# The head of a hybrid encoder layer: two loads of x on ScalarE's queue, transposes moved behind products, one zero product more

## Chip, cores and metric

One core of one Trainium2 chip. The metric is the device time of one execution in microseconds (us). The kernel is written in the direct style: each engine has its own program, and semaphores order them.

## What is computed

One layer (DEPTH = 1) of an encoder over 512 tokens of 1024 channels, in float32: RMS norm, one projection `h @ w_in` to 7 blocks of 512 columns and 3072 gate logits, three branches (chunked softmax attention, stick-breaking attention, multi-scale pooling), a gated sum through `w_out`, then a gated MLP with a convolution of width 3.

```
def rms_norm(x, gain):
    y = xf * lax.rsqrt(jnp.mean(xf * xf, axis=-1, keepdims=True) + EPS)
    return (y * gain.astype(jnp.float32)).astype(x.dtype)
...
        h = rms_norm(x, norm_mix[l])
        proj = h @ w_in[l]
        q_a, k_a, v_a, q_b, k_b, v_b, u_c, g_logits = jnp.split(proj, IN_SPLITS, axis=-1)
...
        x = x + merged @ w_out[l]
        h2 = rms_norm(x, norm_ffn[l])
        x = x + conv_gated_mlp(h2, w_up[l], conv_w[l], conv_b[l], w_down[l])
```

## The kernel before

Every large product is made of three matmuls in the type float32r. Both operands are split into a high part (a copy rounded to float32r, by ACT) and a low part (the rest, by DVE), and `product` (L1607 to L1611) adds hi x lo, hi x hi and lo x hi in PSUM. Weights come in units of 128 x 1024 floats, 512 KB, through two slots of `w_raw`: SP loads a unit in two transfers, ACT writes `w_hi`, DVE writes `w_lo` and counts up `lo_ready`, and PE waits for that.

Only the **head**, the first 24 us or so, is touched. There x has no transposed form yet. x lies in `x_in` as four blocks of 128 tokens (t = 0 to 3), and each block is loaded in two halves of 512 channels (g = 0 and 1), 256 KB each (`x_load`, L291 to L294), with a semaphore of its own, `x_landed[t][g]`. PE transposes a half with four matmuls against the identity (`x_transposes`, L1638 to L1647), ACT copies the result to `xt_hi` (`xt_split_hi`, L544), DVE writes `xt_lo` (`xt_split_lo`, L985).

The first products are those of the values of branch A, with the transposed x as the stationary operand. The first unit holds two slices of 512 columns of `w_in`, for channels 0 to 127 and 128 to 255. Here they are called the **first and the second slice**. The first is one transfer (L313, semaphore `first_landed`), the second two transfers of 64 partitions each (L315). ACT multiplies each with the norm's gain on its way to `w_hi` (`first_hi`, L563), DVE does the same for `w_lo` (`first_lo`, L991). For token block 0, PE needs the first slice for `kk = 0` and the second for `kk = 1`; token blocks 1 to 3 follow with two products each.

The order of each engine is written out by hand. PE: three zero products (`warm(0)`, zeros from `h_lo` into a bank that is written over later), the transposition of the gains, the transposes of block 0, three more zero products (`warm(1)`, count in `WARM`), the transposes of block 1, and then in turn product and transposes, so that the sets of blocks 2 and 3 follow the first and second product of block 0. ACT: load of the gains (`g_row`, L537), table load, first slice, block 0, second slice, blocks 1 to 3. DVE: `g_mix`, first slice, block 0, second slice, blocks 1 to 3. SP issues all other loads: block 0 of x, first slice, second slice, blocks 1 to 3, the next unit, the second halves of x, and, when DVE has done the second slice (`lo_ready` at 1), the unit after that.

Of the kernel before, what the change touches and what calls it, by code (L numbers as in the profile page):

```python
# [22 lines left out]
TT = S // P  # L23
# [4 lines left out]
WB = 512  # L28
# [44 lines left out]
QK0_BANK, SS0_BANK = 2, 4  # L73
SS_BANK = 6
MIX = 4
WARM = (3, 3)


def build(nc, x, norm_mix, w_in, b_gate, q_norm_a, k_norm_a, rel_bias_a, w_pool, pool_scale,
          w_branch_a, w_branch_b, w_branch_c, w_out, norm_ffn, w_up, conv_w, conv_b, w_down, out):  # L80
    ctx = ExitStack()
    with ctx:
# [3 lines left out]
        def sem(name):  # L86
            return ctx.enter_context(nc.semaphore(name))

        def region(kb, *specs):


            with ExitStack() as scope:
                if kb:
                    scope.enter_context(nc.sbuf_tensor(f"below_{specs[0][0]}", [P, 256 * kb], FP32))
                return [scope.enter_context(nc.sbuf_tensor(n, s, d)) for n, s, d in specs]
# [36 lines left out]
        x_in, = region(64, ("x_in", [P, TT, D], FP32))  # L132
# [51 lines left out]
        x_landed = [[sem(f"x_landed{t}_{g}") for g in range(2)] for t in range(TT)]  # L184
# [62 lines left out]
        def x_turned(t):  # L247

            return ps[:, X_BANKS[t], :].rearrange("p (k c) -> p k c", c=P)
# [22 lines left out]
        xw = x[0].rearrange("(t p) d -> p t d", p=P)  # L272
# [17 lines left out]
        def _(sp):  # L290
            def x_load(t, g):  # L291

                c = slice(g * WB, g * WB + WB)
                sp.dma_start(x_in[:, t, c], xw[:, t, c]).then_inc(x_landed[t][g], 16)  # L294
# [13 lines left out]
            def values(n, u, c0):  # L308
                load(n, u % 2, [win_c[:, 2 * u + i:2 * u + i + 1, c0:c0 + WB] for i in range(2)])
# [3 lines left out]
            sp.dma_start(w_raw[:, 0, 0:WB], win_v0[:, 0, :]).then_inc(first_landed, 16)  # L313
            for r in (slice(0, HD), slice(HD, P)):
                sp.dma_start(w_raw[r, 0, WB:UNIT], win_v0[r, 1, :]).then_inc(w_landed[0], 16)  # L315
            for t in range(1, TT):
                x_load(t, 0)
            values(N_VA + 1, 1, V_A * P)
            for t in range(TT):
                x_load(t, 1)  # L320
# [200 lines left out]
        def _(act_e):  # L521
            a = act_e
# [12 lines left out]
                act(w_hi[:, slot, :], w_raw[:, slot, :], ACT.Copy).then_inc(hi_ready, 1)  # L535

            a.dma_start(g_row[:, :], norm_mix[0].rearrange("(k c) -> k c", c=P)).then_inc(gmix_landed, 16)  # L537
            a.preload_act_table_set("natural_log_exp_and_others")
            a.wait_ge(const_ready, 1)

# [1063 lines left out]
        def _(pe):  # L1604
# [21 lines left out]
            def warm(i):  # L1626


                for _ in range(WARM[i]):
                    mm3(ps[:, V_A_BANKS[0], :], ones_heads[:, :], h_lo[:, 0, :], start=True, stop=True)  # L1630
# [7 lines left out]
            def x_transposes(t, g):  # L1638

                pe.wait_ge(x_landed[t][g], 16)  # L1640
                if g == 1:
                    pe.wait_ge(xt_lo_ready, t + 1)
                if (t, g) == (2, 0):
                    pe.wait_ge(gmix_ready, 1)
                for k in range(4 * g, 4 * g + 4):
                    last = nc.tensor.transpose(x_turned(t)[:, k % 4, :], x_in[:, t, k * P:k * P + P], ident[:, :])  # L1646
                last.then_inc(xt_rest_done if g else xt_done, 1)  # L1647

            def value_product(bank, k, t, c, slot):

                tk = slice(t * P, t * P + P)
                return product(ps[:, bank, :], xt_hi[:, k, tk], xt_lo[:, k, tk], w_hi[:, slot, c], w_lo[:, slot, c],
                               k == 0, k == KD - 1)
# [10 lines left out]

            x_transposes(0, 0)
            warm(1)
            x_transposes(1, 0)
            for t in range(TT):
                pe.wait_ge(xt_lo_ready, t + 1)
                for kk in range(2):  # L1670
                    if t == 0:
                        pe.wait_ge(lo_ready if kk else first_lo_ready, 1)
                    last = value_product(V_A_BANKS[t], kk, t, slice(kk * WB, kk * WB + WB), 0)
                    if t == 0:
                        x_transposes(kk + 2, 0)
            last.then_inc(unit_done, 1)
            for t in range(TT):
                x_transposes(t, 1)
# [353 lines left out]
```

## Time and profile before

| | us |
|---|---|
| median of 3 runs | 823.93 (823.73 to 824.07) |
| profiled execution, device time | 822.09 |
| its span, first to last instruction | 820.2 |
| PE busy | 813.5 |
| DVE busy | 606.3 |
| ACT busy | 407.4 |
| DMA, mean rate | 138 GB/s |

The span is 1.9 us shorter than the profiled execution's device time. Times inside the trace are counted from the start of the span. Busy time of PE is that of matmuls, which overlap in the pipeline; where a line has a start, the distance between two starts says what a matmul takes.

### The profile page before, as it was taken

How to read it: one execution, taken by the hardware profiler on the slowest of the kernel's cores; microseconds unless marked ns; L12 is line 12 of the kernel's file. 1: busy time of each engine (PE TensorE's matmuls, PEld its weight loads, DVE VectorE, ACT ScalarE, POOL GpSimd, SP SyncE). 2: the span in 40 equal slices, each digit the busy share in tenths (PEclk: the TensorE clock that was granted, in tenths of full speed). 3: DMA queues.
4: the chain of work that ended last, by engine and by line, in shares of the span. 5: the costliest groups of instructions: out<-in, count | busy, mean ns of one | idle time of the engine just before them, and what ended most of it. 6: DMA issues, size and time to landing. Idle time of an engine off the chain costs nothing.

```text
span 820.2 us, 11715 instructions
## 1 busy us (share of the span) xinstructions
PE 813.5 (99%) x3863; PEld 675.8 (82%) x3863; DVE 606.3 (74%) x893; ACT 407.4 (50%) x572; POOL 24.1 (3%) x42
## 2 busy tenths in 40 slices
PE   8999999999999999999999999999999999999998
PEld 6888888888888888888888888888888888888886
DVE  5958888868668775555554578777777878898797
ACT  6547676656545545434341464334433444565653
POOL 1010000000000060000000000000000000000000
PEclk9999999999999999999999999999999999999999
DMA  6342333222222223333367523665655555576454
GB/s 210 103 130 78 96 85 100 80 63 67 77 77 77 69 73 90 102 91 102 90 219 245 190 78 103 205 193 191 201 190 188 180 185 188 172 221 210 149 182 173
DMA packets 130702, 113.26 MB, mean 138 GB/s; under 512 B 6148, under 2 KB 109544, under 8 KB 129264
## 3 DMA queue, kind: packets, MB, share of 16 engines
q1 hardware_dynamic: 129840, 110.63, 43.0%
q0 software_dynamic: 672, 2.12, 0.9%
q8 instruction: 16, 0.26, 0.1%
q10 hardware_dynamic: 160, 0.14, 0.0%
q14 instruction: 14, 0.11, 0.0%
HBM read 99.21 MB, written 13.65 MB: 138 GB/s over the span
## 4 chain that ended last, share of the span: by engine, by line
PE 98%; DMA 1%; DVE 0%; SPq 0%; issue 0%; DVEq 0%
PE ps L1609 30%; PE ps L1610 30%; PE ps L1611 30%; PE ps L1741 2%; PE ps L1731 2%; PE ps L1756 1%; PE ps L1755 1%; DMA x_in<-in_x_dram 1%; PE ps L1909 0%; DVE out_sb L1594 0%; PE ps L1646 0%; PE ps L1705 0%; PE ps L1724 0%; PE ps L1706 0%; SPq L315 0%
## 5 line engine op out<-in xcount | busy, mean ns | idle before, releaser
L1609 PE MATMUL ps<-h_lo,w_hi 128*128 128x512 f32 x704 | 276.6, 393 | 0.1
L1611 PE MATMUL ps<-h_hi,w_lo 128*128 128x512 f32 x704 | 274.1, 389 | 0.0
L1610 PE MATMUL ps<-h_hi,w_hi 128*128 128x512 f32 x704 | 274.1, 389 | 0.0
L971 DVE TENSOR_TENSOR w_lo<-w_raw,w_hi 128x1024 fp32r<-128x1024 f32 x112 | 138.0, 1232 | 108.0 <-ACT w_hi L535 79.2
L535 ACT ACTIVATE w_hi<-w_raw 128x1024 fp32r<-128x1024 f32 x96 | 101.7, 1060 | 201.7 <-PE ps L1611 201.6
L1611 PEld LDWEIGHTS ps<-h_hi,w_lo 128*128 128x128 f32 x704 | 132.2, 188 | 27.9
L1609 PEld LDWEIGHTS ps<-h_lo,w_hi 128*128 128x128 f32 x704 | 132.2, 188 | 27.4 <-issue 0.3
L1610 PEld LDWEIGHTS ps<-h_hi,w_hi 128*128 128x128 f32 x704 | 132.3, 188 | 26.3
L1456 DVE TENSOR_TENSOR conv_in<-ps,r_ffn 128x512 f32<-128x512 f32 x44 | 30.3, 690 | 23.9 <-PE ps L1611 22.1
L890 ACT ACTIVATE conv_out<-conv_in,par 128x512 f32<-128x512 f32 x44 | 35.5, 806 | 9.7 <-DVE conv_in L1456 9.7
L1444 DVE SCALAR_TENSOR_TENSOR conv_out<-conv_in,par,conv_out 128x512 f32<-128x512 f32 x44 | 33.1, 752 | 5.0 <-DVE conv_out L1441 1.1
L1441 DVE SCALAR_TENSOR_TENSOR conv_out<-conv_in,par,conv_out 128x512 f32<-128x512 f32 x44 | 32.8, 746 | 1.0 <-ACT conv_out L890 0.9
L529 ACT ACTIVATE w_hi<-w_raw 128x1024 fp32r<-128x1024 f32 x16 | 16.9, 1058 | 29.3 <-PE ps L1611 29.3
L1609 PE MATMUL ps<-w_lo,a_hi 128*128 128x512 f32 x78 | 30.4, 389 | 0.0
L1610 PE MATMUL ps<-w_hi,a_hi 128*128 128x512 f32 x78 | 30.4, 389 | 0.0
L1611 PE MATMUL ps<-w_hi,a_lo 128*128 128x512 f32 x78 | 30.3, 389 | 0.0
L1609 PE MATMUL ps<-h_lo,a_hi 128*128 128x512 f32 x76 | 29.6, 389 | 0.0
L1610 PE MATMUL ps<-h_hi,a_hi 128*128 128x512 f32 x76 | 29.6, 389 | 0.0
L1611 PE MATMUL ps<-h_hi,a_lo 128*128 128x512 f32 x76 | 29.6, 389 | 0.0
L1173 DVE TENSOR_TENSOR pt_lo<-ps,pt_hi 128x1280 fp32r<-128x1280 f32 x16 | 23.9, 1491 | 6.1 <-ACT pt_hi L683 5.9
L1146 DVE TENSOR_TENSOR_SCAN suffix<-keep 128x512 f32<-128x512 f32 (+3 forms) x32 | 23.8, 807 | 4.4 <-ACT keep L667 4.2
L1500 DVE TENSOR_TENSOR w_lo<-w_raw,w_hi 128x1024 fp32r<-128x1024 f32 (+1 forms) x22 | 24.2, 1100 | 3.0 <-ACT w_hi L908 3.0
(238 smaller groups left out, 1304.1 us busy)
## 6 DMA issues: line engine op xcount, KB each, us to landing
w_raw<-in_w_in_dram SPq DMA_DIRECT2D x103, 256.0 KB, 3.1
w_raw<-in_w_up_dram SPq DMA_DIRECT2D x88, 256.0 KB, 3.2
raw_t<-in_w_down_dram SPq DMA_DIRECT2D x11, 1024.0 KB, 8.7
down_sums<-t_sum SPq DMA_DIRECT2D x11, 1024.0 KB, 5.7
w_raw<-in_w_down_dram SPq DMA_DIRECT2D x33, 256.0 KB, 3.0
w_raw<-down_sums SPq DMA_DIRECT2D x33, 256.0 KB, 3.9
w_raw<-in_w_out_dram SPq DMA_DIRECT2D x16, 256.0 KB, 3.2
w_raw<-down_sums SPq DMA_DIRECT2D x22, 128.0 KB, 3.0
```

The lines of the kernel that those rows point to most:

```text
L535: act(w_hi[:, slot, :], w_raw[:, slot, :], ACT.Copy).then_inc(hi_ready, 1)
L890: act(conv_out[:, e, :], conv_in[:, e, 2:2 + S], ACT.Identity, scale=pcol(CW2, j + KF * gv), bias=pcol(CB, j + KF * gv)).then_inc(tap_init, 1)
L971: v.tensor_tensor(w_lo[:, slot, :], w_raw[:, slot, :], r32(w_hi[:, slot, :]), ALU.subtract)\
L1146: last = v.tensor_tensor_scan(rev(suffix, e, n), rev(keep[h], c, n), rev(keep[h], c, n), 1.0, ALU.mult, ALU.bypass)
L1173: v.tensor_tensor(pt_lo[:, :], scores_of(h, 0, SCORES), r32(pt_hi[:, :]), ALU.subtract).then_inc(pt_lo_ready, 1)
L1441: v.scalar_tensor_tensor(out=conv_out[:, e, :], in0=conv_in[:, e, 1:1 + S], scalar=pcol(CW1, j + KF * gv), in1=conv_out[:, e, :], op0=ALU. ...
L1444: v.scalar_tensor_tensor(out=conv_out[:, e, :], in0=conv_in[:, e, 0:S], scalar=pcol(CW0, j + KF * gv), in1=conv_out[:, e, :], op0=ALU.mult ...
L1456: v.tensor_tensor(conv_in[:, e, 2:2 + S], ps[:, e, :], r_ffn[:, :], ALU.mult).then_inc(cin_ready, 1)
L1500: v.tensor_tensor(d_wlo[e][:, u, 0:wide], d_raw[e][:, u, 0:wide], r32(d_whi[e][:, u, 0:wide]), ALU.subtract)\
L1609: mm3(dst, l_hi, r_lo, start=start, stop=False, **kw)
L1610: mm3(dst, l_hi, r_hi, start=False, stop=False, **kw)
L1611: return mm3(dst, l_lo, r_hi, start=False, stop=stop, **kw)
```

## The change

SP no longer issues the first halves of blocks 1 and 2 of x; ACT issues them, behind its load of the gains and ahead of its table load. On PE the transposes of block 1 go behind the first product, and those of blocks 2 and 3 both behind the second. The second batch of zero products has four in place of three.

```
-WARM = (3, 3)
+WARM = (3, 4)
...
-            for t in range(1, TT):
-                x_load(t, 0)
+            x_load(3, 0)
...
             a.dma_start(g_row[:, :], norm_mix[0].rearrange("(k c) -> k c", c=P)).then_inc(gmix_landed, 16)
+
+            for t in (1, 2):
+                a.dma_start(x_in[:, t, 0:WB], xw[:, t, 0:WB]).then_inc(x_landed[t][0], 16)
             a.preload_act_table_set("natural_log_exp_and_others")
...
             warm(1)
-            x_transposes(1, 0)
             for t in range(TT):
                 pe.wait_ge(xt_lo_ready, t + 1)
                 for kk in range(2):
                     if t == 0:
                         pe.wait_ge(lo_ready if kk else first_lo_ready, 1)
                     last = value_product(V_A_BANKS[t], kk, t, slice(kk * WB, kk * WB + WB), 0)
-                    if t == 0:
-                        x_transposes(kk + 2, 0)
+                    if t == 0 and kk == 0:
+                        x_transposes(1, 0)
+                    elif t == 0:
+                        x_transposes(2, 0)
+                        x_transposes(3, 0)
```

PE's order at the start of the program, before. The rows with `ones_heads` are zero products, those with `ident,x_in` are the four transposes of one block, and three rows with `xt_hi` or `xt_lo` are one product:

```order
L1630 MATMUL ps<-h_lo,ones_heads 128x512 x3
L1646 MATMUL ps<-ident,x_in 128x128 x4
L1609 MATMUL ps<-w_lo,xt_hi 128x512
L1610 MATMUL ps<-w_hi,xt_hi 128x512
L1611 MATMUL ps<-w_hi,xt_lo 128x512
L1646 MATMUL ps<-ident,x_in 128x128 x4
L1609 MATMUL ps<-w_lo,xt_hi 128x512
L1610 MATMUL ps<-w_hi,xt_hi 128x512
L1611 MATMUL ps<-w_hi,xt_lo 128x512
L1646 MATMUL ps<-ident,x_in 128x128 x4
```

The same place with the change (lines of the changed kernel are two higher there):

```order
L1632 MATMUL ps<-h_lo,ones_heads 128x512 x4
L1611 MATMUL ps<-w_lo,xt_hi 128x512
L1612 MATMUL ps<-w_hi,xt_hi 128x512
L1613 MATMUL ps<-w_hi,xt_lo 128x512
L1648 MATMUL ps<-ident,x_in 128x128 x4
L1611 MATMUL ps<-w_lo,xt_hi 128x512
L1612 MATMUL ps<-w_hi,xt_hi 128x512
L1613 MATMUL ps<-w_hi,xt_lo 128x512
L1648 MATMUL ps<-ident,x_in 128x128 x8
```

The first product no longer stands behind the transposes of block 1, and the second has one set of transposes ahead of it instead of two.

SP's order at the start, before (L294 is x, L313 the first slice, L315 the second, L303 units):

```order
L294 DMA x_in<-in_x_dram 128x512
L313 DMA w_raw<-in_w_in_dram 128x512
L315 DMA w_raw<-in_w_in_dram 64x512 x2
L294 DMA x_in<-in_x_dram 128x512 x3
L303 DMA w_raw<-in_w_in_dram 128x512 x2
```

ACT's order at the start with the change (L539 is new; L565 splits the slices, L546 the blocks of x):

```order
L536 DMA g_row<-in_norm_mix_dram 8x128
L539 DMA x_in<-in_x_dram 128x512 x2
L540 ACT_TABLE_LOAD
L565 ACTIVATE w_hi<-w_raw,g_mix 128x512
L546 ACTIVATE xt_hi<-ps 128x4x128
L565 ACTIVATE w_hi<-w_raw,g_mix 128x512
```

SP's three loads of x behind the slices become one, and ACT has the two others ahead of its table load.

## Rows read from the trace of the kernel before

**Rows 1.** The page: busy time of the engines, and the chain that ended last.

```profile
PE 813.5 (99%) x3863; PEld 675.8 (82%) x3863; DVE 606.3 (74%) x893; ACT 407.4 (50%) x572; POOL 24.1 (3%) x42
...
PE 98%; DMA 1%; DVE 0%; SPq 0%; issue 0%; DVEq 0%
```

**Rows 2.** Stretches: length, busy PE, PEld, DVE, ACT, POOL; granted clock, DMA share, GB/s.

```profile
2.19:7.30 5.11, 4.17 (x11) 2.58 (x11) 1.52 (x3) 2.40 (x4) 0.78 (x3) 1.00 0.86 273
7.30:24.00 16.70, 16.70 (x88) 14.20 (x89) 12.36 (x24) 12.76 (x24) 0.00 (x0) 1.00 0.61 205
24.00:820.00 796.00, 792.65 (x3766) 659.01 (x3764) 591.50 (x863) 391.61 (x545) 22.06 (x27) 1.00 0.44 136
```

**Rows 3.** What PE waited for: total us, times, longest.

```profile
PE ps L1646 <- DMA x_in<-in_x_dram: 0.9, 1, 0.9
```

**Rows 4.** Timeline of PE: start, us, instruction, idle time before it.

```profile
7.30 0.66 PE L1646 MATMUL ps<-ident,x_in 128*128 128x128 f32 x4 [0.94 <-DMA x_in<-in_x_dram]
7.72 0.47 PE L1609 MATMUL ps<-w_lo,xt_hi 128*128 128x512 f32 x1
8.03 0.39 PE L1610 MATMUL ps<-w_hi,xt_hi 128*128 128x512 f32 x1
8.26 0.40 PE L1611 MATMUL ps<-w_hi,xt_lo 128*128 128x512 f32 x1
...
8.85 0.47 PE L1609 MATMUL ps<-w_lo,xt_hi 128*128 128x512 f32 x1
```

**Rows 5.** Timeline of ACT, the same columns.

```profile
0.88 0.60 ACTq L537 DMA_DIRECT2D g_row<-in_norm_mix_dram  x1
1.51 1.28 ACT L538 ACT_TABLE_LOAD   x1 [1.51 <-PEq L2022]
4.83 0.72 ACT L563 ACTIVATE w_hi<-w_raw,g_mix 128x512 fp32r<-128x512 f32 x1 [2.03 <-DMA w_raw<-in_w_in_dram]
...
6.71 0.72 ACT L563 ACTIVATE w_hi<-w_raw,g_mix 128x512 fp32r<-128x512 f32 x1 [0.68 <-DMA w_raw<-in_w_in_dram]
8.00 0.60 ACT L544 ACTIVATE xt_hi<-ps 128x512 fp32r<-128x512 f32 x1 [0.57 <-PE ps L1646]
```

**Rows 6.** Timeline of DVE.

```profile
6.34 0.69 DVE L985 TENSOR_TENSOR xt_lo<-ps,xt_hi 128x512 fp32r<-128x512 f32 x1
7.46 0.75 DVE L991 SCALAR_TENSOR_TENSOR w_lo<-w_raw,g_mix,w_hi 128x512 fp32r<-128x512 f32 x1 [0.44 <-ACT w_hi L563]
```

**Rows 7.** Timeline of SP, its issues; the last two from windows inside one issue.

```profile
1.34 0.42 SPq L313 DMA_DIRECT2D w_raw<-in_w_in_dram  x1
1.81 1.20 SPq L315 DMA_DIRECT2D w_raw<-in_w_in_dram  x2
...
3.06 0.59 SPq L294 DMA_DIRECT2D x_in<-in_x_dram  x1
...
3.69 0.43 SPq L294 DMA_DIRECT2D x_in<-in_x_dram  x1
```

**Rows 8.** Issues one by one, us to landing: x blocks 1, 2; second slice's halves.

```profile
x_in<-in_x_dram SPq DMA_DIRECT2D x1, 256.0 KB, 4.2
...
w_raw<-in_w_in_dram SPq DMA_DIRECT2D x1, 128.0 KB, 3.2
...
w_raw<-in_w_in_dram SPq DMA_DIRECT2D x1, 128.0 KB, 4.3
```

**Rows 9.** Timeline of PE, the zero products of the second batch.

```profile
5.31 1.05 PE L1630 MATMUL ps<-h_lo,ones_heads 128*128 128x512 f32 x2
...
5.74 0.63 PE L1630 MATMUL ps<-h_lo,ones_heads 128*128 128x512 f32 x1
```

**Rows 10.** Stretches of the DMA, the columns of rows 2.

```profile
2.50:2.75 0.25, 0.25 (x1) 0.19 (x1) 0.00 (x0) 0.25 (x1) 0.25 (x2) 1.00 0.98 369
2.75:3.00 0.25, 0.25 (x2) 0.22 (x1) 0.00 (x0) 0.05 (x1) 0.23 (x1) 1.00 0.79 230
3.00:3.25 0.25, 0.25 (x2) 0.11 (x1) 0.00 (x0) 0.00 (x0) 0.00 (x0) 1.00 0.67 213
...
4.25:5.25 1.00, 1.00 (x5) 0.96 (x5) 0.00 (x0) 0.42 (x1) 0.00 (x0) 1.00 0.74 96
```

## Prediction

> **What bounds the kernel now.** I read the profile page first. PE is busy for 813.5 of 820.2 us and the chain that ended last is 98% PE [rows 1], so only time in which PE stands still, or work added to it, can move the end. Next I read the table by stretches [rows 2]. From 7.30 to 24 us PE is busy for all 16.70 us, and after 24 us it is idle for 796.00 - 792.65 = 3.35 us in all. The idle time that an edit of the head can reach is therefore ahead of 7.30 us. The list of what PE waited for agrees: behind the kernel's first instructions it has one entry, 0.9 us for a piece of x [rows 3]. The change is about that one. A shift of PE's work at 7.30 us arrives at the end one for one, because nothing behind it waits for anything but PE.
>
> The third view is the timeline of PE, ACT and DVE up to 10 us [rows 4 to 6]. The reader is to see two chains in it. **Chain one**: the first slice of w_raw lands and ACT splits it at 4.83 and block 0 of x behind it, DVE starts its lo part at 6.34 and ends it at 6.34 + 0.69 = 7.03. From about 7.05 (an engine starts some 0.02 to 0.03 after its releaser) PE has all it needs for the first product, but it stands at the transposes of block 1, whose x lands only at 7.26 (issued at 3.06, 4.2 to landing [rows 7, 8]). **Chain two**: the second slice lands, ACT starts on it at 6.71, DVE works from 7.46 to 7.46 + 0.75 = 8.21, and only then may the second product run.
>
> **The change on PE.** Two matmuls of a product start 0.23 apart (8.03 and 8.26), so a product takes 3 x 0.23 = 0.69; from one product to the next, with a set of four transposes between them, it is 8.85 - 7.72 = 1.13, which leaves 0.44 for the set [rows 4]. Nothing is added there but the zero product, and nothing is removed; the order alone changes. Let d be the time by which the first slice lands later than before, and e the same for the second slice.
> - PE starts the first product at 7.05 + d in place of the transposes at 7.30.
> - The transposes of block 1 start at 7.74 + d and take 0.66 to their end at 8.40 + d. ACT needs 0.04 + 0.60, DVE 0.03 + 0.69 and PE 0.03, so the third product may start at 9.79 + d.
> - The second product starts at the later of 7.05 + d + 0.69 + 0.44 = 8.18 + d and 8.21 + e. Behind it are 0.69 and two sets of transposes, 0.88, so the third product may also not start before 9.75 + d or 9.78 + e.
> - Before, the third product started at 9.97 (read off the second at 8.85, with 0.69 + 0.44 behind it).
>
> So PE's whole stream moves by the larger of **d - 0.18 and e - 0.19**. The most that can be won is 0.18 us, with d = e = 0; the idle time of 0.94 that the trace shows can't be won whole, since chain one ends at 7.03 whatever x does.
>
> **The zero product.** The second and third zero product of the second batch start at 5.31 and 5.74, and the last one takes 0.63 [rows 9]. The spacing of 0.43 against the 0.23 of the same shape after 7.30 says that PE works at the 1.2 GHz level there and at 2.4 GHz from 7.30 on (the column of the granted clock shows 1.00 in both stretches, so it has no record of the first one [rows 2]). A fourth one would start near 6.16 and end by 6.80, or sooner if the clock rises ahead of it. It lies in the gap up to 7.05 and costs nothing; if the cover were gone it would cost 0.43.
>
> **The two loads.** SP loses two issues (0.59 and 0.43 [rows 7]); all that stands behind them on SP is issued about 1.0 us earlier. ACT gets them behind its load of the gains (0.88 to 1.48), so at about 1.5 and 2.0, where SP had them at 3.06 and 3.69. Queued behind them on ACT is the table load, 1.28, which would end at about 2.5 + 1.28 = 3.8 in place of 2.79. It is hidden: ACT then waits 2.03 for the first slice until 4.83 [rows 5]. Should each issue take the 0.60 of the gains' load, it ends at 4.0, still hidden.
>
> What the two loads do to d and e is the unknown. Before, the first slice (issued by SP at 1.34) had only block 0 of x ahead of it, and the second slice (two issues from 1.81 on [rows 7]) nothing of x behind the first slice. Now 256 KB of block 1 are asked for at 1.5, and 256 KB of block 2 at 2.0, in the same time. At the best rate here, 369 GB/s, 256 KB are 0.71 us [rows 10]. **Bounds of d**: none (the second queue is served behind), and 0.71 (all of block 1 goes ahead). The DMA was not full from 2.75 to 3.25 (230 and 213 GB/s [rows 10]), which leaves room for some 70 KB, 0.2 us. I take d = 0.45, near the upper end less that room. **Bounds of e**: none, and the time until block 2 landed before, since by then the same five transfers were all in: 3.69 + 4.2 = 7.89 [rows 8] against 6.71, so 1.2; with both blocks wholly ahead and today's slow stretch unchanged, 1.4. The slow stretch from 4.25 to 5.25, where the DMA is 74% busy but moves 96 GB/s, lies on the second slice: its second half landed 4.3 us after its issue, its first 3.2 [rows 8, 10]. A part of block 2 can move during it at no cost to the slice. I take e = 0.5, in the lower half for that reason.
>
> The rows show no case of two queues that are both full, so they can't say who is served first. The Trainium skill ("DMA: Bandwidth & Descriptors", Queues, rings and completion order) says that each DMA engine takes turns between the queues that have work for it, packet by packet, and the section on issuing engines adds that a second issuing engine saves only the time of issuing. That speaks against this change: by it both transfers of equal size end together, d is at its upper end of about 0.7 and the sum would be 0.5 instead of 0.3. No row here tests it.
>
> **Behind the head.** The other loads of SP, the second halves of x and the next unit among them, are issued 1.0 us earlier and have no more bytes ahead of them than they had; PE waits for none of them up to 24 us [rows 2], and it needs them 0.2 us earlier at most. The unit after that is behind the same wait as before, the second slice's lo part on DVE, and moves by e. Cost: nothing.
>
> **Sum.** The larger of 0.45 - 0.18 = 0.27 and 0.5 - 0.19 = 0.31: PE's stream is 0.3 us later. The profiled execution took 822.09 us, span 820.2, so the same execution with the change would take 822.4. The median of the runs shown is 823.93, 1.84 above it; the same 0.3 on it gives **824.2 us**. Bounds by the unknowns: 823.75 (no delay) to 825.1 (e = 1.4). A difference of 0.2%, 1.65 us, is about what a measurement of this kernel can tell from no change, so nearly all of this is "the same".
>
> **Rivals.**
> - **No delay at all, or the second queue does nothing of what it should** (it is served only when SP's has no work): 823.75, within 0.2%. For it: ACT's loads are asked for later than the first slice. Against: both are in flight together, at a DMA that is 98% busy [rows 10]. 24%.
> - **Long delay of the second slice**: by the skill's turns and with block 2 wholly ahead, shifts of 0.8 to 1.6 us, up to 825.5; within 0.2%. 15%.
> - **Slower**, one mechanism: the second slice waits behind both blocks (1.4) and a second slow stretch as that at 4.25 falls on it, worth the 4.3 - 3.2 = 1.1 us that today's one shows. e = 2.5, and the time is 823.93 + 2.3 = 826.2. It decides from e = 1.85 on (1.65 + 0.19 us). For it: such a stretch is there in the only trace. Against: one has to come on top. 6%.
> - **Faster through the clock.** In the trace the clock is up by 7.30, behind an idle gap of 0.94. The timed runs are 1.84 us longer than the profiled one. Were that because PE stays at 1.2 GHz for longer in them (about eight matmuls of the head at 0.43 in place of 0.23 are 1.6), the fourth zero product and the shorter gap could give it back: 823.93 - 1.84 = 822.1. The skill ("TensorE: Matmul & The Clock Gate", Part 1) says that the clock rises after sustained work and that the moment varies from run to run, which would allow it. Against: the three runs lie within 0.34 us, where a moment that varied would scatter them. 5%.
>
> **Chances.** The forecast's case, a shift of 0.05 to 0.8 us, has 50%; with 24% and 15% beside it, the same within 0.2% has 89%, slower 6%, faster 5%. Range for 8 in 10: from the no-delay case less the scatter of the runs (some 0.3 to 0.4) to the middle of the long-delay case: 823.3 to 825.3.
>
> **What would show it.** In the profile of the changed kernel: PE's first product stands ahead of the transposes of block 1 and starts between 7.1 and 7.8, not at 7.72 behind them; ACT's first split starts at 4.83 + d with d from 0 to 0.71; its second at 6.71 + e; four zero products end ahead of the first product; PE's wait for x is gone, and a wait for DVE's w_lo or xt_lo stands in its place. The end shifts by the larger of d - 0.18 and e - 0.19. I am wrong if PE waits later than 10 us in the head, if block 0 of x lands late behind ACT's loads, or if the time moves by over 1.6 us with this stretch unchanged.

## The result and the profile after

The median of 22 executions is 824.94 us (823.19 to 827.18), that of the kernel before, run beside it, 823.73 us (821.89 to 824.36). The ratio is 1.0018 with a 95% interval of 1.001 to 1.0026, or 0.8 to 2.1 us: slower, by about 0.2%. That is clear of the noise, and at the edge of what the prediction called the same. This ratio and those below lie nearer to the ratio of the means (824.77 against 823.29 here) than to that of the medians; for a kernel whose executions fall into groups, as will be seen, the median jumps when one group passes a half. The profiled execution took 825.44 us (span 823.6), against 822.09 and 820.2 before.

Both sets of executions are wider than the three that stood ahead of the prediction. The kernel before falls into two groups. Of 33 executions measured with the first experiments, 11 lie from 821.9 to 822.4 and 22 from 823.4 to 824.3, with nothing between. The profiled execution of before belongs to the lower group, and all three runs of the table to the upper one. With the change, 7 executions lie from 823.2 to 823.9, 4 from 824.3 to 824.8 and 11 above 825; 10 of these 11 have a mean granted clock of 0.997 or 0.998, which none of before had in the experiments below. In other sets a few executions of before do lie between the groups (822.58 and 822.67 among the 22 above).

The stretches after, with the same columns as [rows 2]:

```profile
2.19:7.30 5.11, 4.60 (x12) 2.91 (x12) 1.31 (x3) 2.49 (x3) 0.77 (x3) 1.00 0.96 278
7.30:24.00 16.70, 15.26 (x73) 12.82 (x74) 9.37 (x15) 11.50 (x21) 0.00 (x0) 0.90 0.51 173
24.00:823.60 799.60, 795.99 (x3781) 661.68 (x3779) 594.98 (x874) 393.18 (x549) 22.32 (x27) 1.00 0.44 136
```

Up to 24 us PE is idle for 1.44 us where it was idle for nothing, and the granted clock is 0.90 in that stretch. After 24 us PE is idle for 3.6 us, where it was 3.4. Where the clock was low is shown by a stretch of its own:

```profile
10.46:13.87 3.41, 3.41 (x13) 2.92 (x12) 0.91 (x2) 1.19 (x3) 0.00 (x0) 0.50 0.98 349
```

From 10.46 to 13.87 us the granted clock is 0.50, that is 1.2 GHz, with PE busy all the time. Ahead of it PE had stood still twice. The list of what PE waited for, against [rows 3]:

```profile
PE ps L1611 <- DVE w_lo L993: 1.2, 1, 1.2
PE ps L1611 <- DVE xt_lo L987: 0.8, 1, 0.8
```

PE's timeline, against [rows 4]:

```profile
4.74 2.06 PE L1632 MATMUL ps<-h_lo,ones_heads 128*128 128x512 f32 x4
7.57 0.49 PE L1611 MATMUL ps<-w_lo,xt_hi 128*128 128x512 f32 x1 [0.78 <-DVE xt_lo L987]
...
8.37 0.60 PE L1648 MATMUL ps<-ident,x_in 128*128 128x128 f32 x4
10.13 0.54 PE L1611 MATMUL ps<-w_lo,xt_hi 128*128 128x512 f32 x1 [1.17 <-DVE w_lo L993]
10.48 0.63 PE L1612 MATMUL ps<-w_hi,xt_hi 128*128 128x512 f32 x1
10.90 0.63 PE L1613 MATMUL ps<-w_hi,xt_lo 128*128 128x512 f32 x1
11.33 1.91 PE L1648 MATMUL ps<-ident,x_in 128*128 128x128 f32 x8
12.89 0.77 PE L1611 MATMUL ps<-w_lo,xt_hi 128*128 128x512 f32 x1
...
13.88 0.39 PE L1613 MATMUL ps<-w_hi,xt_lo 128*128 128x512 f32 x1
14.11 0.40 PE L1611 MATMUL ps<-w_lo,xt_hi 128*128 128x512 f32 x1
```

The reader should see the second product at 10.13 where it was at 8.85, and then the spacing: 0.42 between 10.48 and 10.90 instead of 0.23. ACT's timeline has the cause of the first of these, against [rows 5]:

```profile
1.51 0.84 ACTq L539 DMA_DIRECT2D x_in<-in_x_dram  x2
2.38 1.28 ACT L540 ACT_TABLE_LOAD   x1 [2.38 <-issue]
5.31 0.72 ACT L565 ACTIVATE w_hi<-w_raw,g_mix 128x512 fp32r<-128x512 f32 x1 [1.65 <-DMA w_raw<-in_w_in_dram]
5.94 0.58 ACT L546 ACTIVATE xt_hi<-ps 128x512 fp32r<-128x512 f32 x1
8.57 0.72 ACT L565 ACTIVATE w_hi<-w_raw,g_mix 128x512 fp32r<-128x512 f32 x1 [2.05 <-DMA w_raw<-in_w_in_dram]
```

The first slice is split at 5.31 instead of 4.83, so d = 0.48. The second is split at 8.57 instead of 6.71, so e = 1.86. The issues one by one, against [rows 8], first the two blocks of x on ACT's queue (issued at 1.51 and 1.91), then the two halves of the second slice:

```profile
x_in<-in_x_dram ACTq DMA_DIRECT2D x1, 256.0 KB, 5.0
...
x_in<-in_x_dram ACTq DMA_DIRECT2D x1, 256.0 KB, 5.9
...
w_raw<-in_w_in_dram SPq DMA_DIRECT2D x1, 128.0 KB, 5.4
...
w_raw<-in_w_in_dram SPq DMA_DIRECT2D x1, 128.0 KB, 6.1
```

The blocks landed at 6.5 and 7.8, the second half of the slice, issued at 2.42, at 8.5. It came in behind both blocks. The packets show how. The list of the DMA's queues has SP's loads as q1 and ACT's as q10. From 4.25 to 5.75 us it reads, before and then after:

```profile
q1 hardware_dynamic: 118, 0.21, 71.2%
...
q10 hardware_dynamic: 213, 0.40, 78.2%
q1 hardware_dynamic: 56, 0.10, 20.8%
```

More than twice as much was moved as before (0.50 MB in place of 0.21), but ACT's queue had 213 of the 269 packets, and SP's, on which the second slice lies, 56 in place of 118. It is the same in all six kernels with both blocks on ACT's queue: that queue has 201 to 223 of 256 to 305 packets.

**The whole of the 3.4 us between the two profiled executions can be placed.** The late slice moves PE's stream by e - 0.19 = 1.67. The second product and the two sets of transposes behind it took 12.89 - 10.13 = 2.76 in place of 0.69 + 0.88 = 1.57, at the low clock: 1.19. The third product took 14.11 - 12.89 = 1.22 in place of 0.69: 0.53. The sum is 3.39.

### The profile page after: what moved, and what is told of

Its sections match the earlier page's. It is cut to its first block, busy times and chain, and to the rows that moved or that the text cites. A ratio compares the mean times of both kernels' runs of the same rounds, so it can differ in the third digit from the quotient of the medians.

```text
span 823.6 us, 11717 instructions
## 1 busy us (share of the span) xinstructions
PE 815.9 (99%) x3864; PEld 677.4 (82%) x3864; DVE 606.5 (74%) x893; ACT 407.2 (49%) x572; POOL 24.4 (3%) x42
## 4 chain that ended last, share of the span: by engine, by line
PE 98%; DMA 1%; DVE 1%; SPq 0%; ACT 0%; issue 0%; DVEq 0%
PE ps L1611 30%; PE ps L1612 30%; PE ps L1613 30%; PE ps L1745 2%; PE ps L1735 2%; PE ps L1760 1%; PE ps L1759 1%; DMA w_raw<-in_w_in_dram 1%; PE ps L1913 0%; PE ps L1648 0%; DVE out_sb L1596 0%; PE ps L1709 0%; PE ps L1728 0%; PE ps L1710 0%; DVE w_lo L993 0%; ACT w_hi L565 0%
## 5 line engine op out<-in xcount | busy, mean ns | idle before, releaser
L1611 PE MATMUL ps<-w_lo,xt_hi 128*128 128x512 f32 x64 | 25.7, 401 | 1.9 <-DVE w_lo L993 1.2
```

What stands on the lines that cost most here:

```text
L1611: mm3(dst, l_hi, r_lo, start=start, stop=False, **kw)
```

## The experiments

The change has three parts: the loads on ACT's queue, the order of PE, and the fourth zero product. Theory A was that the loads hold up the second slice; theory B that the new order costs; theory C that the clock is decided by something else than the loads. The clock had to be tried by itself as well.

**1. The loads back on SP, all else as changed.**

```
-            x_load(3, 0)
+            for t in range(1, TT):
+                x_load(t, 0)
...
-            for t in (1, 2):
-                a.dma_start(x_in[:, t, 0:WB], xw[:, t, 0:WB]).then_inc(x_landed[t][0], 16)
```

> The changed kernel with the two loads of x back on SP; new order of PE and four zero products kept. Theory A (the loads on ACT's queue hold up the second slice, and the order of PE only exposes it): ACT starts on the second slice near 6.7 us again, PE's third product starts near 9.8 (before: 9.97), time 0.1 to 0.3 us below the kernel before. Theory B (the order of PE is itself what costs, since the second product has one set of transposes less ahead of it): the third product later than 9.97 and the time at least 0.8 us above before. Theory C (the clock falls because of the new order, whatever the loads do): the granted clock drops to 1.2 GHz for a stretch and the time is 1 us or more above before.

Measured: 822.12 us (821.93 to 822.65, 11 executions), ratio 0.9986 (0.9977 to 0.9995) to the kernel before. It is faster, by more than expected. In the profiled execution ACT starts on the second slice at 7.02 and the third product starts at 10.19:

```profile
7.02 0.51 PE L1609 MATMUL ps<-w_lo,xt_hi 128*128 128x512 f32 x1 [0.23 <-DVE xt_lo L985]
...
8.59 0.50 PE L1609 MATMUL ps<-w_lo,xt_hi 128*128 128x512 f32 x1 [0.16 <-DVE w_lo L991]
...
10.19 0.47 PE L1609 MATMUL ps<-w_lo,xt_hi 128*128 128x512 f32 x1
```

By e = 7.02 - 6.71 = 0.31 the stream should be 0.12 later than before, and the third product is 0.22 later. That is later than 9.97, as theory B has it, but 0.12 of the 0.22 is the slice's own lateness. PE's stream was not ahead of the profiled one of before, and the median still fell by 1.6 us (the mean by 1.0): all 11 executions lie where only the lower group of before lies. The slice itself starts between 6.69 and 7.02 in the profiles of the six kernels with the slice and x on SP, so 0.3 us of e is scatter. Theories B and C fall as put, and A had the gain too small; the loads cost 824.94 - 822.12 = 2.8 us, and something in the rest of the change gains.

**2. The loads alone.** The kernel before with the two loads moved to ACT.

> The kernel before with only the two loads of x issued by ACT; order of PE and three zero products as before. Theory A: the second slice starts on ACT near 8.6 as with the whole change, its low part is ready near 10.1, so the second product moves from 8.85 to near 10.1; one set of transposes more is done by then, so PE's stream is 1.2 us late, and with a wait of over 1 us the clock may fall in some executions: 1.2 to 2.5 us above before. Theory B: no change to before, within 0.3 us, since the order of PE is that of before.

Measured: 823.36 us (822.95 to 824.3), ratio 0.9999 (0.999 to 1.0008). My expectation failed as a number, since I had set it against the median of before. ACT starts on the second slice at 8.16, e = 1.45, as theory A wants; the fastest execution is 822.95 against 821.9. But the executions form one group (822.95 to 823.75, and one at 824.3), with none 1.7 us above the rest:

```profile
4.73 1.63 PE L1632 MATMUL ps<-h_lo,ones_heads 128*128 128x512 f32 x3
6.16 1.05 PE L1648 MATMUL ps<-ident,x_in 128*128 128x128 f32 x4
7.89 0.79 PE L1611 MATMUL ps<-w_lo,xt_hi 128*128 128x512 f32 x1 [0.67 <-DVE xt_lo L987]
```

Block 1 has landed by the end of the zero products, so PE goes on with its transposes at 6.16 without a gap. By this reading the loads cost about 1 us by the slice and return as much by the filled gap. That is argued from the times. The one profiled execution is the slowest of the 11 (824.3), and in it PE stands still for 0.67 ahead of the first product and the clock comes up late, the gap ahead of the transposes filled or not:

```profile
8.48 0.63 PE L1612 MATMUL ps<-w_hi,xt_hi 128*128 128x512 f32 x1
8.90 0.63 PE L1613 MATMUL ps<-w_hi,xt_lo 128*128 128x512 f32 x1
...
12.46 0.40 PE L1612 MATMUL ps<-w_hi,xt_hi 128*128 128x512 f32 x1
12.70 0.40 PE L1613 MATMUL ps<-w_hi,xt_lo 128*128 128x512 f32 x1
```

**3. The zero product alone.**

```
-WARM = (3, 3)
+WARM = (3, 4)
```

> The kernel before with four zero products in place of three, nothing else. If the zero product only fills the gap up to 7.30: the same as before within 0.1 us. Rival (the clock): the runs of before fall into two groups, near 822.1 and near 823.9; if the later group is that in which the clock rises late, an added zero product moves executions to the lower group, and the median falls by up to 1.7 us.

Measured: 822.27 us (821.73 to 822.58), ratio 0.9988 (0.9979 to 0.9997). The rival holds: one zero product of 0.43 us takes 1.4 us off the median and 1.0 off the mean: none of the 11 executions lies in the upper group. Why it does so is less certain. No execution of the upper group of before was profiled, and no run separates the shorter gap from the added work ahead of it.

**4. The wait filled with five zero products**, behind the transposes of block 1, all else as changed.

```
                         x_transposes(1, 0)
+                        for _ in range(5):
+                            mm3(ps[:, V_A_BANKS[3], :], ones_heads[:, :], h_lo[:, 0, :], start=True, stop=True)
```

> The changed kernel with five more zero products behind the transposes of block 1, in the 1.2 us in which PE waits for the second slice. Their time is 5 x 0.23 = 1.15, so by themselves they cost nothing. Theory A with the clock (the profiled execution of the changed kernel lost 1.7 us to the wait and some 1.7 us more to 3.4 us at 1.2 GHz behind it): the clock stays at 2.4 GHz from its rise on, the wait stays, the slowest executions (825.4) vanish and the median is near 823.7 to 824.5. Rival (the low clock has nothing to do with the idle gap): the share of executions with a low stretch stays about half, and the median stays near 825.

Measured: 824.24 us (823.44 to 828.25), ratio 1.0014 (1.0002 to 1.0027). The median is in the expected place and a mean clock of 0.998 occurs once in 11, but the slowest executions did not vanish: 5 of 11 lie above 825. The profiled one (825.49) shows why:

```profile
4.73 2.06 PE L1632 MATMUL ps<-h_lo,ones_heads 128*128 128x512 f32 x4
7.41 0.79 PE L1611 MATMUL ps<-w_lo,xt_hi 128*128 128x512 f32 x1 [0.63 <-DVE xt_lo L987]
8.00 0.63 PE L1612 MATMUL ps<-w_hi,xt_hi 128*128 128x512 f32 x1
8.43 0.63 PE L1613 MATMUL ps<-w_hi,xt_lo 128*128 128x512 f32 x1
...
9.56 2.48 PE L1678 MATMUL ps<-h_lo,ones_heads 128*128 128x512 f32 x5
11.84 0.44 PE L1611 MATMUL ps<-w_lo,xt_hi 128*128 128x512 f32 x1
```

Here the clock had not risen at all by the first product (8.00 to 8.43 is 0.43), so the five zero products took 2.28 and not 1.15, and pushed the second product to 11.84. Filling the second gap seems to mend a fall of the clock (one low mean clock in 11, where the change has 10 in 22) and makes a late rise worse. The first gap was still open.

**5. The zero product undone** in the changed kernel (3 in place of 4).

> The changed kernel with three zero products again in the second batch. Theory: an idle gap ahead of the first products decides whether the clock is up in time, and the fourth zero product shortens it. Without it the changed kernel stands idle from 6.4 to 7.5: its median rises from 824.9 to 825.5 or more, and fewer than 4 in 11 executions lie below 824. Rival: with the loads on ACT the late second slice decides alone and the zero product does nothing: median 824.5 to 825.2 as with it.

Measured: 824.75 us (823.26 to 826.13, 12 executions), ratio 1.0024 (1.0014 to 1.0033), 4 of 12 below 824. The median did not rise to 825.5, so here the rival holds: with the loads on ACT the fourth zero product changes nothing that can be seen. It still ends at 6.8, while PE's first product has moved from 7.0 to 7.57, so 0.8 us of the gap stays open. In the profiled execution (824.4) the clock is late here too: two matmuls are still 0.43 apart at 8.06 and 8.49.

**6. Only block 1 on ACT's queue.**

> The changed kernel with only block 1 of x on ACT's queue, block 2 on SP behind the second slice. Theory (all that ACT's queue carries goes ahead of the second slice): the slice is late by the 0.7 us of block 1, plus what a slow packet adds, so ACT starts on it near 7.4 to 7.8 in place of 8.6, PE's wait behind the transposes of block 1 falls from 1.2 to about 0.5, and the fastest executions lie near 822.4 to 822.9, median about 823. Rival (any second queue at all causes the delay, by the way the transfers start): the slice starts on ACT at 8.3 or later and the time stays near 824.9.

Measured: 822.55 us (822.23 to 825.03, 12 executions), ratio 1.0004 (0.9994 to 1.0014). ACT starts on the second slice at 7.23, so the delay is about 0.5 or less in place of 1.9, and PE does not wait behind the transposes of block 1. Of the second queue it is the second block that hurts most. The first slice still comes late (5.34), PE stands idle for 0.8 ahead of the first product, and 4 of 12 executions lie from 824.5 to 825.0. They hold the mean at 823.22, above the 823.04 of before, though the median is below.

**7. The second slice on ACT's queue, all of x on SP**, with PE's new order and four zero products.

> The order of PE and the zero product of the change, all of x on SP, and the second slice on ACT's queue. Theory (what ACT's queue carries is served ahead of what SP has queued): the second slice is there by 6.0 to 6.5, the first one later than 4.8 by up to 0.5, and block 1 of x no later than 7.3. PE's first product starts at 7.05 to 7.5; time 822.1 to 822.6. Rival (turns of equal share): the slice and the first slice end together, both near 5.5, first product near 7.8, time 822.7 to 823.2.

Measured: 822.74 us (822.25 to 823.33, 11 executions), ratio 0.9996 (0.9987 to 1.0005). Neither forecast of the slice holds: its halves landed 4.2 and 5.0 us after their issue and ACT starts on it at 7.18, no earlier than on SP (6.69 to 7.02). So it is not shown that ACT's queue goes ahead as a rule: from 4.25 to 5.75 us it has 101 of 246 packets here. What the traces show is that the slice took longer from issue to landing in every kernel with loads beside it on the other queue; with the slice and x on SP its halves took 3.1 to 3.3 and 4.2 to 4.6 us.

**8. One zero product less** than before, nothing else.

> The kernel before with two zero products in the second batch in place of three. Theory (the idle gap ahead of 7.30 decides when the clock rises): the gap grows by 0.43, the lower group of executions near 822.1 gets smaller or vanishes, median 823.8 to 824.5 with nearly all above 823. Rival (a zero product matters only as work, not for the clock): no change to before, a third of the executions near 822.1.

Measured: 823.99 us (822.0 to 824.94), ratio 1.0005 (0.9995 to 1.0015). The median moved by 0.5 in the expected direction, but the interval holds no change. The lower group has 3 of 11 executions, where before has 14 of 35 beside it; with so few the two shares can't be told apart, so the theory is neither borne out nor refuted. Its profiled execution is the slowest of the 11, 824.94, above the upper group of before. It shows what a late rise looks like with the slice and x on SP:

```profile
4.74 1.20 PE L1630 MATMUL ps<-h_lo,ones_heads 128*128 128x512 f32 x2
7.40 1.12 PE L1646 MATMUL ps<-ident,x_in 128*128 128x128 f32 x4 [1.46 <-DMA x_in<-in_x_dram]
...
10.30 0.78 PE L1609 MATMUL ps<-w_lo,xt_hi 128*128 128x512 f32 x1
10.88 0.63 PE L1610 MATMUL ps<-w_hi,xt_hi 128*128 128x512 f32 x1
11.30 0.63 PE L1611 MATMUL ps<-w_hi,xt_lo 128*128 128x512 f32 x1
...
13.35 0.40 PE L1611 MATMUL ps<-w_hi,xt_lo 128*128 128x512 f32 x1
13.59 0.40 PE L1609 MATMUL ps<-w_lo,xt_hi 128*128 128x512 f32 x1
```

After an idle gap of 1.46 the spacing is still 0.42 at 10.88 to 11.30, and 0.24 only from 13.35 on. In [rows 4] it was 0.23 at 8.03. That the upper group of before is such a late rise is argued from here, not seen.

**9. PE's order undone**, loads and zero product kept.

> The changed kernel with PE's order of before: loads on ACT and the fourth zero product kept, transposes of block 1 ahead of the first product, of block 2 ahead of the second. Theory (the new order exposes the late second slice, since one set of transposes less is ahead of it and PE stands still twice): PE is busy with zero products and transposes without a gap to about 7.2 us, no execution is late by the clock, and the time is that of the loads alone, 823.0 to 823.6 (median 823.36 there), with no value above 824.5. Rival (the order does nothing, the loads do all): median near 824.9, spread to 826 as with the whole change.

Measured: 823.45 us (823.0 to 826.55, 12 executions), ratio 1.0008 (0.9998 to 1.0018). The median is as the theory says, and 10 of 12 lie from 823.0 to 823.7; two (824.68 and 826.55) lie above the bound I gave. PE was not busy without a gap either: in the profile it waits 0.49 ahead of the first product and 0.96 for the slice, with the clock at 2.4 GHz in both products (matmuls 0.23 and 0.24 apart). With the loads on ACT, the new order costs 824.94 - 823.45 = 1.5 us.

**10. The order alone.**

> The kernel before with PE's new order alone: loads on SP, three zero products. By the sum of the prediction the stream moves by 0.18 us to the front at most; and the idle gap ahead of it shrinks from 0.94 to about 0.65. If the gap decides about the clock: two groups as before, the lower one at 821.9 to 822.2 with a larger share than the third or so of before, median 822.2 to 823.5. Rival (the order alone is worth as much as the fourth zero product): all executions below 822.7. Rival (it costs): median above 824.

Measured: 823.34 us (821.96 to 824.2), ratio 1.0001 (0.9991 to 1.001), 5 of 12 in the lower group, whose fastest is not below that of before. That is the share of before beside it (12 of 29), and the gap ahead of the first product did not shrink to 0.65 but stayed at 0.94, since the clock rose during the zero products, which took 1.32 us in place of 1.63 and ended early. The order gains nothing by itself. In its profiled execution the third product starts at 9.85 (before: 9.97): 0.12 of the 0.18 that the prediction had as the most to win.

**11. Five zero products**, loads on SP, new order.

> The loads on SP, the new order and five zero products in place of four. The fifth one starts near 6.6 and ends near 7.2, so that it closes the gap but pushes the first product from 7.02 to about 7.2. Theory: nothing more is to be had of the clock, since four are enough for all executions: 822.1 to 822.4, 0.1 to 0.2 above the 822.12 with four. Rival (the remaining spread of 821.9 to 822.65 is the clock's as well): below 822.0 with a smaller spread.

Measured: 822.25 us (821.82 to 822.8), ratio 0.9991 (0.9983 to 1.0). Nothing more is to be had; this kernel, the one of the first experiment and the one of the third can't be told apart.

**12. Six zero products in the changed kernel**, so that the first gap is closed and the second left open.

> The changed kernel with six zero products in the second batch in place of four, so that PE is busy without a gap from 4.7 to the first product near 7.5; the wait of 1.2 us for the second slice stays. Theory (two costs apart: the late slice, and the clock, which needs PE to be busy ahead of the first product): the clock's part vanishes, no execution shows a mean clock of 0.998 or less or lies above 824.5, and what is left is the slice, 823.3 to 823.9, 1.2 to 1.7 above the 822.12 with the loads on SP. Rival (the second wait, behind the transposes of block 1, is what drops the clock): a good part of the executions stays at 0.997 to 0.998 and above 825, median above 824.2.

Measured: 823.62 us (823.11 to 824.16, 11 executions), ratio 1.0005 (0.9996 to 1.0014), and no mean clock below 0.999. The theory's times and clocks hold. One number does not: the wait for the slice was to stay at 1.2 and is 0.54 in the profile.

```profile
4.73 2.91 PE L1632 MATMUL ps<-h_lo,ones_heads 128*128 128x512 f32 x6
7.44 0.79 PE L1611 MATMUL ps<-w_lo,xt_hi 128*128 128x512 f32 x1
8.02 0.45 PE L1612 MATMUL ps<-w_hi,xt_hi 128*128 128x512 f32 x1
8.30 0.39 PE L1613 MATMUL ps<-w_hi,xt_lo 128*128 128x512 f32 x1
...
9.67 0.50 PE L1611 MATMUL ps<-w_lo,xt_hi 128*128 128x512 f32 x1 [0.54 <-DVE w_lo L993]
```

PE is busy from 4.73 to the first product, the clock rises during it (0.58 to the second matmul, then 0.28), and the wait for the slice, 0.54 here, does not bring it down. That wait is half of the changed kernel's, because the slice is split at 8.11 here, 0.46 earlier, and the transposes behind the first product start later (8.53 in place of 8.37). So the run shows that six zero products remove the slow executions, but not which of the two gaps brings the clock down. What is left of the change against the first experiment is 823.62 - 822.12 = 1.5 us, the late slice; the clock's part was 824.94 - 823.62 = 1.3 us, late rises and falls together.

The eight combinations, medians in us (measured at four different times, beside which before had 823.5 to 823.8):

| | nothing else | order | zero product | both |
|---|---|---|---|---|
| loads on SP | 823.5 to 823.8 | 823.34 | 822.27 | 822.12 |
| two loads on ACT | 823.36 | 824.75 | 823.45 | 824.94 |

## Why the prediction was right and where it was not

The time lies in the range, and the direction is the forecast's: 824.94 against 824.2. The shift of 1.2 us is not the forecast's own case (0.05 to 0.8, at 50%) but that of the rival with the long delay (0.8 to 1.6, at 15%). That the median came so near is partly luck, since the terms that were off (the slice, the zero product and the clock) cancel in part. Step by step:

- **The form of the sum was right.** PE's stream moves by the larger of d - 0.18 and e - 0.19, the second product waits for the slice's low part, and the wait for x is replaced by waits for `xt_lo` and `w_lo`, as written. With d = 0.48 and e = 1.86 it gives 1.67, and the profile's 3.4 us are this and the low clock.
- **d was sized right**: 0.45 predicted, 0.48 measured in the changed kernel (0.33 to 0.80 in the six kernels with both loads on ACT).
- **e was mis-sized**: 0.5 predicted, with 1.2 and 1.4 as upper bounds; 1.86 measured, above both. In the six kernels with both loads on ACT, ACT started on the second slice at 8.03 to 8.73, e = 1.3 to 2.0. I had taken the lower half because block 2 could move in the slow stretch at no cost to the slice. The blocks did move there, but, as far as the packets tell, at the slice's cost: from 4.25 to 5.75 us SP's queue had 56 packets in place of 118, ACT's 213. The bounds took the order of landing as given, with the slice no later than the last block; it landed behind both. Why ACT's queue got that share is not settled. A lower rate of the whole DMA does not explain e: from 5.75 to 8.25 it was 268 GB/s after and 345 before, but over all the profiles it was 268 to 327 with both blocks on ACT and 295 to 345 with the slice and x on SP, and experiment 2, at 327, has e = 1.45.
- **The rule of turns between the queues** (the Trainium skill, "DMA: Bandwidth & Descriptors", Queues, rings and completion order) would have given d of about 0.7 and equal ends. The measured d of 0.48 is below that, and the second slice ended 0.7 us behind the last block rather than beside it, with 213 of 269 packets on ACT's queue from 4.25 to 5.75 us. Both slices were late, so the rule's direction was right, and an equal sharing is not what this trace shows. What the Trainium skill says in the same page under "Issuing engines are not separate DMA queues", that a second issuer saves only the time of issuing, agrees: the DMA moved 278 GB/s in the stretch up to 7.30, where it was 273.
- **The zero product was costed at nothing**, with the idle gap as its cover. The cover was there, and it was the wrong question. Alone it is worth -1.4 us; with the loads on ACT nothing can be seen of it (824.75 and 824.94, 823.36 and 823.45). I had the mechanism among the rivals, at 5% and a price of up to 1.84. What I held against it, that three runs within 0.34 us leave no room for a clock that varies, was an argument from three draws out of the upper group. The 1.84 us between the profiled execution and the median is the distance of two groups, and the sum carried it along unexplained.
- **The clock could also fall.** No rival had an idle PE bring back 1.2 GHz after the rise. The profiled execution of the changed kernel does that, and by their mean clock (0.997 or 0.998) 9 others of the 22 do. With the late rises it is 1.3 us of the median.
- The table load, the 1.0 us that SP's other loads gained, and the unit behind them cost nothing, as predicted: PE waits for none of them in any of the kernels that I profiled.

The small total, then, is the difference of terms larger than itself: about -1.4 us for the zero product, about +1.5 for the late slice and +1.3 for the clock (by the means -1.0, +1.4 and +1.1). The forecast of +0.3 had only the slice in it, at a fifth of its size. Without the clock's part the total would have been about nothing (experiment 12: ratio 1.0005, 0.9996 to 1.0014), so the sign and the nearness of the forecast are in part luck.

The version that beats both kernels is the change without its loads: 822.12 us, 2.8 us below the change and 1.6 below the kernel before (ratio 0.9986, 0.9977 to 0.9995; by the means 2.6 and 1.0 us). The zero product alone gives the same within the intervals.

## What to carry to other kernels

A few runs of one kernel may all come from one of two groups; when the profiled execution and the median differ by more than the runs scatter, look for what makes two groups before costing anything. An idle gap of PE ahead of its first real work may cost more than its own length, since the clock may come up late behind it or fall (argued here from the times and a few traces), and a product of zeros that looks like it only fills the gap can be the best part of a change. A load that is moved to another queue to come earlier makes another one come later: ask which one, and whether it is needed first.

## What the runs showed of the hardware

- The moment at which PE's clock rises differs between executions of nearly the same head. By the spacing of matmuls it was up by 5.7 us in experiment 11 (0.23 from 5.69 on), by 8.03 us in the profiled execution of before, at about 13.2 with one zero product less, and at about 11.8 in experiment 4, with starts of PE that agree to 0.01 us up to the second batch of zero products at 4.74. The granted clock's column reads 1.00 over stretches ahead of the rise in which the spacing is 0.42 to 0.43 (9.50 to 11.84 us in experiment 4, for one), so for the head the spacing has to be read, not the column.
- After a rise, PE's waits of 0.8 and 1.2 us between 6.8 and 10.1 us were followed by a granted clock of 0.50 from 10.46 to 13.87, with PE fully busy. Waits of 0.49 and 0.96 us (experiment 9) and of 0.54 us (experiment 12) were not, in the profiled executions, nor one of 0.94 us in experiment 10, where the clock had risen by 6 us.
- The second 128 KB half of the second slice landed 4.2 to 4.6 us after its issue in the six kernels with the slice and x on SP, 4.8 with 256 KB beside it on ACT's queue, and 5.6 to 6.3 in the six with 512 KB there.
- With 512 KB on ACT's queue, that queue had 201 to 223 of 256 to 305 packets from 4.25 to 5.75 us; with 256 KB it had 86 of 289, and SP's queue 203, more than its 118 before.
